# Two layer norms in eight groups of 256 columns, rests formed on VectorE from PSUM, one weight split moved

## The reference

```python
def layer_norm(x, g, b):
    mu = jnp.mean(xf, axis=-1, keepdims=True)
    var = jnp.mean(jnp.square(xf - mu), axis=-1, keepdims=True)
    return (xf - mu) * lax.rsqrt(var + LN_EPS) * g + b
...
mix = hybrid_mixer(x, ...)                              # ends in mixed @ w_o
x = layer_norm(DEEPNORM_ALPHA * x + mix, ln1_gain, ln1_bias)
xa = memory_cross_attention(x, mem, w_mq, w_mkv, w_mo)  # begins with x @ w_mq, ends in o @ w_mo
x = layer_norm(DEEPNORM_ALPHA * x + xa, ln2_gain, ln2_bias)
ff = peer_ffn(x, w_pq, sub_keys, expert_u, expert_v)    # begins with x @ w_pq
x = layer_norm(DEEPNORM_ALPHA * x + ff, ln3_gain, ln3_bias)
```

## Time and profile before

| | us |
|---|---|
| median of 3 runs | 2421.46 (2420.43 to 2421.61) |
| the profiled execution | 2421.28 |
| its span | 2419.5 |
| TensorE busy | 2333.2 (96%) |
| VectorE busy | 1684.4 (70%) |
| ScalarE busy | 1106.1 (46%) |
| GpSimd busy | 649.6 (27%) |

### The profile page before, as it was taken

The page is one execution under the profiler, slowest core; times in us unless marked ns, Lnnn a source line. Parts: engine busy times, 40 slices in busy tenths (PEclk is TensorE's granted clock), DMA queues, the critical chain, the costliest instruction groups (busy, mean ns, idle before and its releaser), DMA issues.

```text
span 2419.5 us, 45242 instructions
## 1 busy us (share of the span) xinstructions
PE 2333.2 (96%) x14770; PEld 2106.2 (87%) x14770; DVE 1684.4 (70%) x2628; ACT 1106.1 (46%) x1716; POOL 649.6 (27%) x425
## 2 busy tenths in 40 slices
PE   7999999999899979999999999999999999999996
PEld 7988799878897779999999999999788888888885
DVE  4444556655644555799999999998577767777556
ACT  3444455543433333345544454454444444444442
POOL 0000000000201020778877786565100000000100
PEclk9999999999899989999999999999999999999998
DMA  8788544565354545677878787777888878887763
GB/s 316 250 278 265 188 140 148 162 220 192 134 178 122 193 133 140 149 188 187 189 187 187 186 188 189 186 189 198 282 293 286 282 250 283 285 289 273 242 220 122
DMA packets 333365, 507.60 MB, mean 210 GB/s; under 512 B 69072, under 2 KB 216784, under 8 KB 325744
## 3 DMA queue, kind: packets, MB, share of 16 engines
q1 hardware_dynamic: 285856, 443.79, 58.8%
q0 software_dynamic: 46736, 62.17, 11.0%
q10 hardware_dynamic: 704, 0.75, 0.1%
HBM read 485.33 MB, written 21.23 MB: 209 GB/s over the span
## 4 chain that ended last, share of the span: by engine, by line
PE 83%; DVE 7%; DMA 4%; issue 3%; SPq 1%; ACT 1%; DVEq 0%; POOL 0%; ACTq 0%; POOLq 0%
PE ps L703 28%; PE ps L460 18%; PE ps L671 17%; PE ps L466 15%; DVE u_lo L1430 3%; DMA u_raw<-in_peer_u_dram 3%; PE ps L660 1%; DVE u_turned L1424 1%; SPq L383 1%; DMA temps<-gates_scratch 1%; PE ps L608 1%; PE ps L626 1%; DMA weight_ring<-in_w_in_dram 0%; DVE split_ring L1217 0%; PE ps L644 0%
## 5 line engine op out<-in xcount | busy, mean ns | idle before, releaser
L671 PE MATMUL ps<-parts,u_hi 128*128 128x240 f32 x3904 | 670.2, 277 | 7.0 <-DVE u_lo L1430 4.6
L1217 DVE TENSOR_TENSOR split_ring<-weight_ring,split_ring 128x1024 fp32r<-128x1024 f32 x288 | 353.2, 1233 | 365.9 <-ACT split_ring L788 364.8
L671 PEld LDWEIGHTS ps<-parts,u_hi 128*128 128x128 f32 x3904 | 586.6, 189 | 18.3 <-DVE u_lo L1430 14.5
L1160 POOL DMA_INDIRECT gates_scratch<-sb_gains x256 | 520.1, 2032 | 170.5 <-issue 99.1
L703 PE MATMUL ps<-parts,temp_parts 128*128 128x512 f32 x2304 | 545.8, 390 | 5.5 <-DVE parts L1566 5.5
L671 PE MATMUL ps<-parts,u_lo 128*128 128x240 f32 x1952 | 536.2, 275 | 0.0
L703 PEld LDWEIGHTS ps<-parts,temp_parts 128*128 128x128 f32 x2304 | 434.0, 188 | 96.7 <-DVE parts L1566 6.3
L788 ACT ACTIVATE split_ring<-weight_ring 128x1024 fp32r<-128x1024 f32 x288 | 302.9, 1059 | 368.5 <-PE ps L460 226.1
L460 PE MATMUL ps<-split_ring,parts 128*128 128x512 f32 x1920 | 439.9, 391 | 5.6 <-DVE parts L1333 3.9
L460 PEld LDWEIGHTS ps<-split_ring,parts 128*128 128x128 f32 x1920 | 360.8, 188 | 80.9 <-DVE split_ring L1217 4.1
L973 ACT ACTIVATE u_hi<-u_turned 128x1024 fp32r<-128x1024 f32 x244 | 258.9, 1061 | 342.8 <-DVE u_turned L1424 341.4
(11 more groups left out here) (222 smaller groups left out, 1414.1 us busy)
## 6 DMA issues: line engine op xcount, KB each, us to landing
u_raw<-in_peer_u_dram SPq DMA_DIRECT2D x1024, 128.0 KB
region<-in_peer_v_dram SPq DMA_DIRECT2D x256, 512.0 KB, 4.5
weight_ring<-in_w_in_dram SPq DMA_DIRECT2D x96, 512.0 KB, 5.0
weight_ring<-in_w_mkv_dram SPq DMA_DIRECT2D x64, 512.0 KB, 3.8
gates_scratch<-temps POOLq DMA_DIRECT2D x16, 1024.0 KB, 7.4
weight_ring<-in_w_o_dram SPq DMA_DIRECT2D x32, 512.0 KB, 3.7
weight_ring<-in_w_mq_dram SPq DMA_DIRECT2D x32, 512.0 KB, 3.7
weight_ring<-in_w_mo_dram SPq DMA_DIRECT2D x32, 512.0 KB, 3.6
```

The lines of the kernel that those rows point to most:

```text
L671: m = nc.tensor.matmul(ps[:, b, 0:ET], u[:, c], x[kk][:, 0:ET], start=kk == 0 and n == 0, stop=kk == KB - 1 and n == 2)
L1160: pool.indirect_dma_start(gates_by_one, bass.IndirectOffsetOnAxis(ap=idx_all[:, j:j + 1], axis=0), gate_all[:, j:j + 1], None, compute_op= ...
L1217: nc.vector.tensor_tensor(w_lo[j % SPLIT], raw[j % RAW], w_hi[j % SPLIT].bitcast(F32), ALU.subtract).then_inc(lo_ready, 1)
```

## The change

The norms work in eight groups of 256 columns. `normalize(g)` makes one group; VectorE then normalizes group g + 1, and forms the rest of group g itself, straight from PSUM (`turned_lo`, as the kernel does it at its start), which raises `turned_taken`. GpSimd's subtractions and the whole copies of the first norm are gone; the second norm's whole copy into xw stays on ScalarE, behind the rest of its group, and raises `xw_copied`. TensorE transposes groups 0 and 1, then alternates slice g with group g + 2. ScalarE and VectorE split slices 4 to 7 in between. The rest of slice 3 of the following pair, which stood between the last residual and its statistics, is made after the first group's rest. The residual is one instruction per tile, the statistics wait per tile, and the loops of `residual` and of the w_mq section on ScalarE are written out. SyncE's store of x2 waits for 16 groups (both norms), which is the same point, the end of the second norm.

```diff
@@ -368,3 +367,3 @@
             load_query_weights(0, range(12))
-            sp.wait_ge(x_ready, 2 * NP)
+            sp.wait_ge(x_ready, 16)
             sp.dma_start(x2_dram, r5[:, :]).then_inc(spilled, 16)
...
@@ -588,16 +587,21 @@
 
-            def turn_norm(src, nth, first_chunk, pair, acts, chunks):
+            def turn_norm(src, nth, done, pair, acts):
 
-                for g in range(8):
-                    if g % chunks == 0:
-                        pe.wait_ge(x_ready, first_chunk + g // 2 + chunks // 2)
+                def turn_group(g):
+                    pe.wait_ge(x_ready, done + g + 1)
+                    if done and g >= 4:
+                        pe.wait_ge(xw_copied, g - 3)
                     turn(src, g, nth + g)
-                    if g in (3, 7):
-                        pe.wait_ge(turned_lo_ready, nth - 16 + g // 2 + 1)
-                        slices("cols", range(g // 2 - 1, g // 2 + 1), pair, acts, 0, 1)
-                pe.wait_ge(turned_taken, nth + 8)
-                pe.wait_ge(turned_lo_ready, nth - 8)
 
-            turn_norm(x1, 16, 0, MQ0, x1T, 2)
-            rest_of_pair(MQ0, x1T)
+                turn_group(0)
+                for g in range(8):
+                    if g == 0:
+                        turn_group(1)
+                    pe.wait_ge(turned_taken, nth + g + 1)
+                    slices("cols", [g], pair, acts, 0, 1)
+                    if g + 2 < 8:
+                        turn_group(g + 2)
+
+            turn_norm(x1, 16, 0, MQ0, x1T)
+            panel("cols", 1, MQ0, x1T)
             section("cols", MQ0 + 1, NP // 2 - 1, x1T)
...
@@ -635,3 +639,3 @@
             pe.wait_ge(keysT_copied, 1)
-            turn_norm(x2, 24, 4, PQ0, x2T, 4)
+            turn_norm(x2, 24, 8, PQ0, x2T)
 
...
@@ -648,3 +652,4 @@
             for pair in range(PQ0, PQ0 + NP // 2):
-                slices("cols", range(4 if pair == PQ0 else 0, NS), pair, x2T, 0, 1)
+                if pair > PQ0:
+                    slices("cols", range(NS), pair, x2T, 0, 1)
                 slices("cols", range(8, 10), pair, x2T, 1, 1)
...
@@ -766,3 +771,8 @@
 
-            def copy_turned_whole(dst, nth, whole_of):
+            def copy_turned_norm(nth, pair, whole=None):
+
+                def copy_whole(g):
+                    act.wait_ge(turned_taken, nth + g + 1)
+                    nc.scalar.activation(whole[:, g * 2 * T:(g + 1) * 2 * T], ps[:, 4 + g % 4, :], ACT.Copy)\
+                        .then_inc(xw_copied, 1)
 
...
@@ -770,8 +780,10 @@
                     act.wait_ge(turned, nth + g + 1)
-                    nc.scalar.activation(dst[:, g * 2 * T:(g + 1) * 2 * T], ps[:, 4 + g % 4, :], ACT.Copy)\
+                    nc.scalar.activation(p1[:, g * 2 * T:(g + 1) * 2 * T], ps[:, 4 + g % 4, :], ACT.Copy)\
                         .then_inc(turned_hi, 1)
-                    if whole_of is whole and g >= 4:
-                        act.wait_ge(turned_lo_ready, g - 3)
-                    nc.scalar.activation(whole_of[g % len(whole_of)], ps[:, 4 + g % 4, :], ACT.Copy)\
-                        .then_inc(turned_taken, 1)
+                    if whole is not None and g > 0:
+                        copy_whole(g - 1)
+                    if 2 <= g < 6:
+                        split_hi(pair, [g + 2])
+                if whole is not None:
+                    copy_whole(7)
 
...
@@ -798,6 +810,6 @@
 
-            def split_pair(pair, take_panel=lambda s: None):
+            def split_pair(pair, take_panel=lambda s: None, first=4):
 
                 for s in range(2):
-                    split_hi(pair, range(4 + 8 * s, 11 + 8 * s))
+                    split_hi(pair, range(first if s == 0 else 12, 11 + 8 * s))
                     take_panel(s)
...
@@ -886,4 +898,6 @@
                 split_pair(pair)
-            copy_turned_whole(p1, 16, whole)
-            section("cols", r0, MQ0, NP // 2, 2 * BANK)
+            copy_turned_norm(16, MQ0)
+            for i in range(NP // 2):
+                split_pair(i + MQ0, lambda s: take("cols", r0, (i * 2 + s) * 2 * BANK, i + MQ0, s, 2 * s),
+                           first=4 if i else 8)
             for h in range(MH):
...
@@ -907,3 +921,3 @@
             nc.scalar.activation(keysT[:, :], ps[:, 7, 0:2 * NKEY], ACT.Copy).then_inc(keysT_copied, 1)
-            copy_turned_whole(p1, 24, [xw[:, g * 2 * T:(g + 1) * 2 * T] for g in range(8)])
+            copy_turned_norm(24, PQ0, xw)
             def copy_scores(n, tk, panels=NP):
...
@@ -939,3 +953,3 @@
                 if i == 0:
-                    split_hi(PQ0, range(4, 11))
+                    split_hi(PQ0, range(8, 11))
                     take_queries(0)
...
@@ -1130,8 +1144,2 @@
                 nc.gpsimd.tensor_tensor(rstd, veps, nhalf[:, 0:NT], ALU.pow).then_inc(rstd_ready, 1)
-                for g in range(8):
-                    hi, lo = [r[:, g * 2 * T:(g + 1) * 2 * T] for r in (p1, p3)]
-                    pool.wait_ge(turned_hi, (n + 2) * 8 + g + 1)
-                    pool.wait_ge(turned_taken, (n + 2) * 8 + g + 1)
-                    src = xw[:, g * 2 * T:(g + 1) * 2 * T] if n else whole[g % 4]
-                    nc.gpsimd.tensor_tensor(lo, src, hi.bitcast(F32), ALU.subtract).then_inc(turned_lo_ready, 1)
                 if n == 0:
...
@@ -1344,23 +1352,26 @@
 
-                with dve.Fori(0, NP // 2) as i:
-                    steps.enter(i, 2)
-                    for s in range(2):
-                        q = i * 2 + s
-                        cols = bass.ds(q * BANK, BANK)
-                        split_lo(i + first_pair, range(4 + 8 * s, 11 + 8 * s))
-                        dve.wait_ge(w_used, (i + first_pair) * PS + (s + 1) * NS)
-                        nc.vector.scalar_tensor_tensor(out=z[:, :, cols], in0=x_old[:, :, cols], scalar=ALPHA,
-                                                       in1=ps[:, 2 * s:2 * s + 2, :], op0=ALU.mult,
-                                                       op1=ALU.add).then_inc(proj_taken, 1)
-                        split_lo(i + first_pair, [11 + 8 * s])
-                        dve.wait_ge(proj_taken, i * 2 + (2 * first_pair + s + 1 + CREDIT))
-                        for t in range(NT):
-                            m = nc.vector.bn_stats(small[:, bass.ds(q * 6 + (65 + t * NP * 6), 6)], z[:, t, cols])
-                        steps.did(m)
-                steps.leave(NP // 2)
+                for q in range(NP):
+                    pair, s = first_pair + q // 2, q % 2
+                    cols = slice(q * BANK, (q + 1) * BANK)
+                    split_lo(pair, range(4 + 8 * s, 11 + 8 * s))
+                    dve.wait_ge(w_used, pair * PS + (s + 1) * NS)
+                    for t in range(NT):
+                        m = nc.vector.scalar_tensor_tensor(out=z[:, t, cols], in0=x_old[:, t, cols], scalar=ALPHA,
+                                                           in1=ps[:, 2 * s + t, :], op0=ALU.mult, op1=ALU.add)
+                        if t == NT - 1:
+                            m.then_inc(proj_taken, 1)
+                        else:
+                            steps.did(m)
+                    if q < NP - 1:
+                        split_lo(pair, [11 + 8 * s])
+                    steps.wait()
+                    for t in range(NT):
+                        if t == NT - 1:
+                            dve.wait_ge(proj_taken, q + (2 * first_pair + 1 + CREDIT))
+                        steps.did(nc.vector.bn_stats(stats[:, t, q, :], z[:, t, cols]))
 
-            def norm(z, dst, nth):
+            def norm(z, dst, nth, turned_before, pair):
 
-                steps.wait()
                 for t in range(NT):
+                    steps.wait(but=NT - 1 - t if t < NT - 1 else 1)
                     steps.did(nc.vector.bn_aggr(mvar[:, t, :], stats[:, t].rearrange("p q c -> p (q c)")))
...
@@ -1369,14 +1380,24 @@
                 dve.wait_ge(gb_landed, (32, 32 + 16 + 128)[nth])
-                for q in range(NP):
-                    cols = slice(q * BANK, (q + 1) * BANK)
+
+                def pieces(a, g):
+
+                    if not nth:
+                        return [a[:, g * T:(g + 1) * T]]
+                    by_block = a.rearrange("p (h q k s) -> p h k q s", h=2, q=4, s=32)
+                    return [by_block[:, g // 4, 2 * (g % 4) + n] for n in range(2)]
+
+                def out_pieces(a, g):
+
+                    if not nth:
+                        return [a[:, g * T:(g + 1) * T]]
+                    return [a[:, (2 * g + n) * P:(2 * g + n + 1) * P].rearrange("p (q s) -> p q s", q=4) for n in range(2)]
+
+                def normalize(g):
+
                     for t in range(NT):
-                        for c, mixed in mixed_parts(q) if nth else [(cols, None)]:
-                            out, z_in, gain = dst[:, t, cols], z[:, t, c], gain_b[:, c]
-                            if nth:
-                                out = by_mixed(dst[:, t])[:, q // 2, :, mixed]
```

(31 more changed lines are left out.)

6 lines of the change are left out of this document (3 added, 3 removed).

## The result

The changed kernel takes 2403.82 us (median of 6 runs, 2401.56 to 2408.24) against 2421.53 for the kernel before (6 runs, 2418.72 to 2423.48): 17.7 us between the medians. The ratio over all runs is 0.9933, with a 95% interval of 0.9923 to 0.9943, which is 16.2 us (13.8 to 18.6). The profiled execution took 2403.12 us with a span of 2401.3, 18.2 less than before. TensorE's busy time hardly moved (2330.7 us, has 2333.2); what went is idle time.

A forecast was written before the change was run, and what follows sets the result against it. TensorE, computing 96% of the span, bounds the kernel; each norm costs it idle time, then half-speed products. Gains of 4.2 + 10.5 = 14.7 us, less 0.2, give 2421.5 - 14.5 = 2407.0 us; range 2401.5 to 2413.5.

The forecast's parts named there:

- the rival in which the clock is spared: Both norms: the clock never drops or returns at once, 2.1 us more gained in each norm, 2402.8 us; chance 0.16.
- hand-overs: Twelve alternations of slices and transpose groups in the norms: 0.2 us taken off the gain.
- (a): Head of each norm: without the rest of slice 3 there, statistics start sooner; gain 1.05 us in each norm.
- (b): First group of 256 columns: TensorE's first transposes at 617.2 instead of 618.79 (norm one), 849.05 instead of 854.00 (norm two).
- (c): Second group and first slice: rest straight from PSUM, GpSimd's subtraction off the chain; slice 0 starts at 619.8 and 851.9.
- (d): Slices 0 to 7 alternate with transpose groups, low clock losing 1.7 us; slice 7 ends at 647.5 and 879.6.
- (e): VectorE in groups 3 to 6: falls back up to 1.4 us within a lead of about 2 us; cost zero.
- (f): ScalarE's whole copies in the second norm, then the split of slice 8: cost zero, 1.4 us to spare.
- (g): SyncE's store of x2 ahead of the query weights: cost zero, slack shrinking from some 16 us to 4.
- (h): GpSimd loses its 16 subtractions in the norms; TensorE's waits on those before the slices were already counted.
- The loops that are written out: The unrolled loops: at most a few instruction fetches, bounded by 1 us.
- The slower side: Eight groups of each norm: the clock stays low throughout, 2455.8 us, 34 us slower than before; chance 0.05.

The follow-up runs named there:

- the filled kernel: The changed kernel with 40 transposes of the identity, result unread, on TensorE behind its stop in each norm; 2398.57 us.
- The two experiments that use up the leads and the slack: The changed kernel with two more VectorE instructions behind the weight split of groups 3 to 6 (2407.47 us), or with x2's picked pieces stored three times (2407.59 us).

## Why the prediction was right

The forecast of 2407.0 us lies 3.2 above the median; its range held. The total alone would mislead: a gain of 17.7 us falls into the band that the prediction gave to the rival in which the clock is spared, and the clock was not spared. The local times show which steps made the gain. They gave 16.6 us where the prediction had 14.7 (14.5 after its hand-overs); the remaining 1.1 of the 17.7 is scatter. By steps:

*(a), the moved split.* 1.05 us forecast. The statistics start 1.24 us behind the stop instead of 2.44, and putting the split back costs 1.1 us at the first transposes in both norms. In norm two VectorE's first (z - mean) steps start 2.71 us behind the stop (840.66) instead of 4.03, 1.3 us sooner. Right, though 0.15 and 0.27 us too small.

*(b), the first group.* 5.5 and 5.1 us to the first transposes, measured 4.97 and 4.73. Here the term was too large. In norm one it is 0.53 us too large: half of that is GpSimd's power, which I took at the 1.15 us of norm one before and which took 0.89, the other half is the earlier head of (a) and a shorter way from the statistics to the power. In norm two the power, taken at 0.88, took 0.73, but it was not what VectorE waited for: the four (z - mean) steps ended last there, as forecast, and most of the 0.35 us is again the earlier head. The steps of 128 columns, a form that the trace before did not have from SBUF, start 0.26 us apart (four in 842.50 to 843.55, where the next kind starts 1.05 later), as extrapolated. The rule of the Trainium skill ("VectorE: DVE Perf Modes", on the TRN2 errata) that pieces should have at least 512 elements names a cost that the rows show too: 0.26, 0.395 and 0.67 us from start to start for 128, 256 and 512 columns, so small pieces are dearer per column. Here that cost lay on an engine with a lead and bought an earlier start.

*(c), the first slice.* 8.1 and 7.9 forecast, 7.5 and 7.3 measured, all of it from (b).

*(d), the alternation.* 3.37 us per slice and group forecast, 3.31 measured, 0.4 us over the norm. Slice 0 was forecast at 4.6 us with bounds of 4.0 and 5.9 around the clock's return; measured 4.33 and 5.37, and 4.22 to 5.47 over all kernels without filling. Against the 3.13 us of the filled kernel the low clock cost slice 0 1.2 and 2.2 us. The forecast of 1.7 for each norm was thus right only as their mean, and that the two errors cancel is luck. Its upper bound of 3.0 has no row behind it: the slowest of the three returns, 5.5 us, gives 2.2. So the local times came to 34.3 and 35.2 instead of 35.9 and 35.6, and the gains to 5.7 and 10.9 us instead of 4.2 and 10.5.

*(e), (f), (g), (h).* VectorE's lead, SyncE's slack and the order of splits were forecast at zero cost, and are: from slice 1 on no row of TensorE shows idle time up to slice 7. The two experiments that use up the leads and the slack bear out leads near 1.85 and 1.05 us, and find a slack of 4.6 us. The loops that are written out cost TensorE nothing either, as the 192.2 us between the two norms, in which they run, are unchanged.

*The rivals.* That the clock never drops did not come about by itself: TensorE stood still from 611.44 and 837.95, and the clock is at its lower level in 615 to 616 and 841 to 842. Made to happen, it is worth 1.5 and 2.1 us a norm, 2.1 forecast. The slower side, low clock through all eight groups, did not occur in any kernel. In the trace after, the Trainium skill's case ("TensorE: Matmul & The Clock Gate", second failure mode), a clock that swings where TensorE pauses briefly between groups of products, did not arise: each slice has two waits in front, but they were already met, TensorE did not pause, and slices 1 to 5 run at 3.11 or 3.12 us. The nearest test is the kernel with more work on VectorE: its two pauses in each norm, of 0.35 to 1.04 us, left slice 5 between them at 3.13 and 3.14 us. So no run here shows the page's case, and none refutes it.

*The totals.* They differ from the local gains by up to 1.7 us (17.7, 15.1, and 21.9 for the filled kernel, against 16.6 and 20.2). The ten timelines show where the scatter lies. Between the two norms every kernel takes 192.1 to 192.2 us; but TensorE's first stop comes between 609.4 and 613.8 us, where all ten kernels give TensorE the same work. It goes with the clock at the kernel's start. The stretch from 10 to 50 us in the changed kernel measured again (first stop 613.41) and in the filled one (609.38); the number before the last two is the clock:

```profile
10.00:50.00 40.00, 33.83 (x238) 33.22 (x237) 18.84 (x25) 16.73 (x20) 0.75 (x1) 0.91 0.88 321
10.00:50.00 40.00, 33.71 (x261) 33.10 (x260) 20.74 (x26) 17.63 (x21) 1.31 (x2) 1.00 0.90 330
```

Over all ten it is 0.91 where the stop comes at 613.4 or later (two kernels), 0.96 at 610.2 to 611.7 (five) and 1.00 at 609.4 or 609.5 (three). Each profile is one execution, and no run changes only this, so the link is read and not proven.

What is open: the shares of group size and order, and why the clock's return moves.

## What to carry to other kernels

Where one engine stands still because another hands over its work in large pieces, price the first piece by the chain up to it and the later ones by whether the supplier keeps its lead; smaller pieces cost the supplier a fixed amount each (0.12 us here), which is free as long as that lead lasts. Measure such a change from the waiting engine's stop to a fixed point of its work, not only by the total. And when a wait of a few microseconds can't be removed, try giving TensorE something to do in it: here 40 transposes of the identity in a wait of 5 us kept the clock up and were worth 1.5 and 2.1 us, more than the 1.1 of the moved weight split.

## What the runs showed of the hardware

GpSimd's power on 128 x 2 elements goes with the form of VectorE's steps beside it: 1.15 us beside steps of 512 columns (first norm before), 0.88 and 0.89 beside steps of 256 (second norm before, first norm after), and 0.73 beside steps of 128 (second norm after). That VectorE works throughout is not what makes it long: in the second norm before, it does.

The interference goes both ways. With GpSimd subtracting, VectorE's two steps of 256 columns took 2.94 us instead of 0.87, and GpSimd's subtraction, 1.40 us in the row beside them, took 2.35 us where it met VectorE's weight split.

The moment at which the clock returns is not fixed by the waits just ahead of it. In the second norm five kernels have the same two waits ahead of slice 0 (4.74 and 0.71 us), and slice 0 takes 4.34, 4.51, 5.32, 5.37 and 5.37 us. A difference of 1 us in one norm of one profile is therefore not a finding.
